# Two transformer-like blocks on one core: loads issued a stage earlier, and one gate projection moved by one pass

## What is computed

```
# block 1: mod = silu(c) @ w_mod + b_mod, six parts of 1024
h = x + g1 * gated_deltanet(rmsnorm(x) * (1 + s1) + b1, ctx likewise)   # 8 heads of 128, two directions
u = rmsnorm(h) * (1 + s2) + b2
h = h + g2 * expert_choice_moe(u)        # 16 experts, hidden 2048, 128 tokens each
# block 2, on x1 = rmsnorm(h) * final_g
p = (rmsnorm(x1) * (1 + s1) + b1) @ w_in
y = [ssd_scan(p), windowed_attention(p)] @ w_out          # 8 scan heads, two directions; sinks, 10 chunks
h2 = x1 + g1 * y
out = rmsnorm(h2 + g2 * grouped_top_k_moe(u2))            # 32 experts, hidden 512, several blocks of 128 tokens
```

## Time and profile before

| | us |
|---|---|
| median of 3 runs | 4617.72 |
| lowest and highest run | 4614.37, 4617.97 |
| the profiled execution | 4615.21 |
| its span on the core | 4613.5 |
| mean granted PE clock | 0.943 |
| PE busy | 4118.3 (89%) |
| DVE busy | 1541.0 (33%) |
| ACT busy | 815.6 (18%) |
| POOL busy | 400.3 (9%) |

### The profile page before, as it was taken

The page is one execution under the profiler, slowest core; times in us unless marked ns, Lnnn a source line. Parts: engine busy times, 40 slices in busy tenths (PEclk is TensorE's granted clock), DMA queues, the critical chain, the costliest instruction groups (busy, mean ns, idle before and its releaser), DMA issues. The chain is left out here.

```text
span 4613.5 us, 42680 instructions
## 1 busy us (share of the span) xinstructions
PE 4118.3 (89%) x14684; PEld 2249.2 (49%) x14684; DVE 1541.0 (33%) x3314; ACT 815.6 (18%) x1818; POOL 400.3 (9%) x385
## 2 busy tenths in 40 slices
PE   6699999998777999999999996997798889999984
PEld 4366666666423444444444443544665344444432
DVE  4577777776352000000000004235953310000003
ACT  2223333332110000000000003111163101011002
POOL 0111111111000000000000000002500010000001
PEclk8799999999888999999999997998799989999997
DMA  6111111110467898888888874010012279999986
GB/s 270 50 27 36 41 41 36 41 30 22 167 256 294 310 313 305 304 313 309 306 308 311 308 264 147 24 29 13 1 70 87 80 254 334 334 335 334 336 312 238
DMA packets 437206, 875.43 MB, mean 190 GB/s; under 512 B 89745, under 2 KB 134625, under 8 KB 430921
## 3 DMA queue, kind: packets, MB, share of 16 engines
q1 hardware_dynamic: 410905, 785.86, 48.8%
q0 software_dynamic: 19616, 71.38, 4.6%
q10 hardware_dynamic: 6544, 16.39, 0.9%
HBM read 801.14 MB, written 72.43 MB: 189 GB/s over the span
## 5 line engine op out<-in xcount | busy, mean ns | idle before, releaser
L1707 PE MATMUL moe_gbank<-moe_ring,moe_xT 128*128 128x512 f32 x1536 | 679.9, 596 | 3.8 <-ACTq L1763 3.8
L1725 PE MATMUL moe_acc<-moe_ring,moe_hidT 128*128 128x512 f32 x1536 | 675.1, 592 | 1.8 <-DVEq L1824 1.1
L1707 PE MATMUL moe_ubank<-moe_ring,moe_xT 128*128 128x512 f32 x1536 | 675.1, 592 | 0.0
L1797 DVE TENSOR_TENSOR moe_hid<-moe_sg,moe_ubank 128x512 f32<-128x512 f32 x96 | 66.0, 688 | 1632.4 <-PE moe_ubank L1707 1632.4
L799 PE MATMUL gdn_pbank<-mix_xT,gdn_w 128*128 128x512 f32 (+1 forms) x1280 | 541.2, 557 | 2.6 <-PEq L693 2.6
L1707 PEld LDWEIGHTS moe_gbank<-moe_ring,moe_xT 128*128 128x128 f32 x1536 | 293.5, 191 | 373.7 <-issue 370.5
L1725 PEld LDWEIGHTS moe_acc<-moe_ring,moe_hidT 128*128 128x128 f32 x1536 | 288.2, 190 | 347.1 <-issue 347.1
L1707 PEld LDWEIGHTS moe_ubank<-moe_ring,moe_xT 128*128 128x128 f32 x1536 | 284.5, 190 | 322.4 <-issue 322.4
L1768 ACT ACTIVATE moe_sg<-moe_gbank 128x512 f32<-128x512 f32 x96 | 57.3, 597 | 1547.6 <-PE moe_gbank L1707 1547.6
L799 PEld LDWEIGHTS gdn_pbank<-mix_xT,gdn_w 128*128 128x128 f32 x1280 | 229.6, 194 | 161.3 <-issue 152.8
L2146 PE MATMUL proj_abank<-mix_yT,mix2x_wq 128*128 128x512 f32 x416 | 180.8, 592 | 0.6 <-PE proj_abank L2146 0.6
(11 more groups left out here) (523 smaller groups left out, 4769.9 us busy)
## 6 DMA issues: line engine op xcount, KB each, us to landing
moe_ring<-in_moe_w_gate SPq DMA_DIRECT2D x64, 2048.0 KB, 7.9
moe_ring<-in_moe_w_up SPq DMA_DIRECT2D x64, 2048.0 KB, 8.2
moe_ring<-in_moe_w_down SPq DMA_DIRECT2D x64, 2048.0 KB, 8.0
moe_ring<-in_w_gate SPq DMA_DIRECT2D x32, 2048.0 KB, 10.5
moe_ring<-in_w_up SPq DMA_DIRECT2D x32, 2048.0 KB, 9.8
moe_ring<-in_w_down SPq DMA_DIRECT2D x32, 2048.0 KB, 10.1
front_wt<-in_w_mod SPq DMA_DIRECT2D x24, 1024.0 KB, 13.8
route_wt<-in_w_ada SPq DMA_DIRECT2D x24, 1024.0 KB, 15.6
```

Of the source, the lines that this page charges most:

```text
L1707: last = nc.tensor.matmul(bank[:], xT[:, k, :], w[:, k * 512:(k + 1) * 512], start=(k == 0), stop=(k == KD - 1))
L1725: last = nc.tensor.matmul(acc[j][:], hidT[:, k, :], w[:, k * D + j * 512:k * D + (j + 1) * 512], start=(f == 0 and k == 0), stop=(f == NF ...
L1797: nc.vector.tensor_tensor(hid[:], sg[:], ubank[:], ALU.mult).then_inc(u_free, 1)
```

## The change

1. The gate projections of head 0 move from iteration 0 into iteration -1, into the same gaps 20 to 27. Iteration 0 has none; from iteration 1 on nothing changes. ACT's SiLU of them moves with them.
2. In iteration 7 SP loads the eight parts of `w_out` when z1 of head 7, the last reader of xT, is done, into xT's space. The wait for the stores leaves `delta_net`; out1's SP waits for them before its load of yk[7], and loads only yk.
3. moe1's last result is computed in a tile of its own at the top of the program (`y_last`, 4 KB in each partition, in front of every other tile but three). POOL no longer waits for the last scatter; n34's SP does, before its loads of x2 and x3, which now come after all six parameters. DVE waits for gain, scale 1 and shift 1, scales, norms the two context tiles, and only then waits for the other three.
4. `project`'s SP issues `a_log`, `dt_bias`, `cap`, `d_skip` and `ssd_norm` before its own loads, and waits for them at its end. tabs and ssd load nothing; `tri` is taken from the top of the program.
5. attention's SP issues, after its own three loads, the 8 loads of w_out_2 and the router's seven. out2 loads no weights; route has no SP block.
6. The stages are nested anew; three that had no semaphores have one or two, and so a block of clears at their end.

The diff, cut to its core:

```diff
 def projections(i):
-    if 0 <= i < H:
-        names += [(f"z{j}", i) for j in range(2)]
+    if i != 0:
+        names += [(f"z{j}", max(i, 0)) for j in range(2)] if i < H else []
...
 # delta_net, SP
+                    if i == H - 1:
+                        sp.wait_ge(p_full, P_AT["z1", i])
+                        for k in range(KD):
+                            sp.dma_start(w_next[:, k, :], w_out[k * P:(k + 1) * P, :]).then_inc(w_ahead, 16)
...
-                sp.wait_ge(y_stored, 16 * H)
...
 # out_norm, SP and PE
                     if yT is None:
+                        if k == KD - 1:
+                            sp.wait_ge(y_stored, 16 * H)
                         sp.dma_start(yk[:, k, :], yT_d[k]).then_inc(w_loaded[k], 16)
-                    sp.dma_start(w[:, k, :], w_out[k * P:(k + 1) * P, :]).then_inc(w_loaded[k], 16)
+                    if w_here is None:
+                        sp.dma_start(w[:, k, :], w_out[k * P:(k + 1) * P, :]).then_inc(w_loaded[k], 16)
...
+                if w_here is not None:
+                    pe.wait_ge(w_ahead, 16 * KD)
                 for k in range(KD):
-                    pe.wait_ge(w_loaded[k], 32 if yT is None else 16)
+                    if yT is None:
+                        pe.wait_ge(w_loaded[k], 16)
...
 # norms_and_narrow, SP and DVE
-                sp.dma_start(gb, row_view(gain)).then_inc(par_loaded, 16)
-                for i in (1, 0):
-                    sp.dma_start(sc[i], row_view(shift_scale[i][1])).then_inc(par_loaded, 16)
-                    sp.dma_start(sh[i], row_view(shift_scale[i][0])).then_inc(par_loaded, 16)
-                    if i:
-                        for t in range(NC_T, NB):
-                            load_x(t)
-                        sp.dma_start(g0, row_view(g_first)).then_inc(par_loaded, 16)
+                sp.dma_start(gb, row_view(gain)).then_inc(ctx_loaded, 16)
+                sp.dma_start(sc[1], row_view(shift_scale[1][1])).then_inc(ctx_loaded, 16)
+                sp.dma_start(sh[1], row_view(shift_scale[1][0])).then_inc(ctx_loaded, 16)
+                sp.dma_start(g0, row_view(g_first)).then_inc(par_loaded, 16)
+                sp.dma_start(sc[0], row_view(shift_scale[0][1])).then_inc(par_loaded, 16)
+                sp.dma_start(sh[0], row_view(shift_scale[0][0])).then_inc(par_loaded, 16)
+                sp.wait_ge(scattered, 16)
+                for t in range(NC_T, NB):
+                    load_x(t)
...
-                dve.wait_ge(par_loaded, 96)
-                for i in (1, 0):
-                    nc.vector.scalar_tensor_tensor(out=sc[i], in0=sc[i], scalar=1.0, in1=gb, op0=ALU.add, op1=ALU.mult)
+                dve.wait_ge(ctx_loaded, 48)
+                nc.vector.scalar_tensor_tensor(out=sc[1], in0=sc[1], scalar=1.0, in1=gb, op0=ALU.add, op1=ALU.mult)
                 dve.drain()
                 for t in range(NC_T):
                     second(t)
+                dve.wait_ge(par_loaded, 48)
+                nc.vector.scalar_tensor_tensor(out=sc[0], in0=sc[0], scalar=1.0, in1=gb, op0=ALU.add, op1=ALU.mult)
+                dve.drain()
...
 # project, SP
+                for tile, rows in scan_parts:
+                    sp.dma_start(tile, rows).then_inc(scan_loaded, 16)
...
+                sp.wait_ge(scan_loaded, 16 * len(scan_parts))
...
 # attention, SP
                 sp.dma_start(snk[:], row_view(sinks)).then_inc(setup, 16)
+                load_next(sp)
...
 # second_block
+            w_next, w_ahead = s1.sb("w_next", [P, KD, D]), s1.sem("w_ahead")
+            def load_next(sp):
+                for k in range(KD):
+                    sp.dma_start(w_next[:, k, :], a["w_out_2"][0][k * P:(k + 1) * P, :]).then_inc(w_ahead, 16)
...
 # program
+        y_last, scattered = top.sb("y_last", [P, D]), top.sem("scattered")
```

More of the change, by code:

```diff
@@ L1250, in tiles_of, with out_norm @@
     return (s, NC_T - 1 - s if s < NC_T else NA - 1 + NC_T - s)
-def out_norm(nc, name, yT_d, w_out, gate, res_rows, h_rows, shift, scale, gain, ident, uT, rows_out, yT=None):
+def out_norm(nc, name, yT_d, w_out, gate, res_rows, h_rows, shift, scale, gain, ident, uT, rows_out, yT=None, w_here=None, w_ahead=None, y_stored=None):
     NBANK = 4
@@ L1257, in out_norm @@
     with Stage(nc, name) as st:
-        w = st.sb("w", [P, KD, D])
+        w = st.sb("w", [P, KD, D]) if w_here is None else w_here
         yk = st.sb("yk", [P, KD, L]) if yT is None else yT
@@ L2271, in scan_tables @@
         with nc.Block() as block:
-            @block.sync
-            def _(sp):
-                sp.dma_start(al[:].rearrange("p d h -> p (d h)"), row_view(a_log.rearrange("d h -> (d h)"))).then_inc(loaded, 16)
-                sp.dma_start(dtb[:].rearrange("p d h -> p (d h)"), row_view(dt_bias.rearrange("d h -> (d h)"))).then_inc(loaded, 16)
             @block.tensor
@@ L2399, in rows @@
                             h = 4 * half + q
-                            last = nc.tensor.matmul(b[:, q * P:(q + 1) * P], dA[:, t, d, h:h + 1].broadcast_to([P, P]), tri[:, d, :], start=True, stop=True)
+                            last = nc.tensor.matmul(b[:, q * P:(q + 1) * P], dA[:, t, d, h:h + 1].broadcast_to([P, P]), tri[:, d * P:(d + 1) * P], start=True, stop=True)
                         last.then_inc(d_full, 1)
@@ L2723, in _, with route @@
                     divide(u)
-def route(nc, hT, w_group, b_group, w_expert, b_expert, cst, ident, ones, idxT, wgt, dest, ebk):
+def route(nc, hT, router, loaded, ident, ones, idxT, wgt, dest, ebk):
     NE = NG + E2
@@ L3150, in second_block @@
-def second_block(nc, a, cst, ident, ones, tri, mod2, h_d, out):
+    with Stage(nc, "ffn1") as ff:
+        idxT, gateT = ff.sb("idxT", [P, E1], U32), ff.sb("gateT", [P, E1])
+        with Stage(nc, "first") as top:
+            xT = top.sb("xT", [P, KD, TOK])
+            w_next = xT[:].rearrange("p k n -> p (k n)")[:, 0:KD * D].rearrange("p (k n) -> p k n", k=KD)
+            w_ahead, y_stored = top.sem("w_ahead"), top.sem("y_stored")
+            with Stage(nc, "mix1") as st:
+                tab = st.sb("tab", [P, H, KINDS, NU])
+                front(nc, consts, (a["w_mod"][0], a["b_mod"][0], a["c"][0], a["c_ctx"], mod1), tile_rows(a["ctx"][0]) + tile_rows(a["x"][0]), a["norm_mix_g"][0],
+                      a["gdn_w_in"][0], a["gdn_a_log"][0], a["gdn_dt_bias"][0], cst, ident[:], xT, tab)
+                delta_net(nc, xT, a["gdn_w_in"][0], a["gdn_conv_w"][0], a["gdn_o_gain"][0], tab, cst, ident[:], ones[:], yT_d, a["gdn_w_out"][0], w_next, w_ahead, y_stored)
+            with Stage(nc, "ffn1r") as s2:
+                uT = s2.sb("uT", [P, KD, L])
+                out_norm(nc, "out1", yT_d, a["gdn_w_out"][0], mod1[0, D6[2]], tile_rows(a["x"][0]), tile_rows(h_d),
+                         mod1[0, D6[3]], mod1[0, D6[4]], a["norm_ffn_g"][0], ident[:], uT, tile_rows(u_d), w_here=w_next, w_ahead=w_ahead, y_stored=y_stored)
+                expert_choice(nc, uT, a["moe_w_router"][0], ident[:], idxT[:], gateT[:], job2)
+        experts(nc, "moe1", E1, F1 // 512, 6, a["moe_w_gate"][0], a["moe_w_up"][0], a["moe_w_down"][0], u_d, idxT[:], ident[:], h_d, gateT=gateT[:], gate=mod1[0, D6[5]], y_last=y_last, last_out=scattered)
@@ L3151, in dram, with second_block @@
+def second_block(nc, a, cst, ident, ones, tri, mod2, h_d, out, scattered):
     def dram(name, shape, dt=F32):
@@ L3184, in second_block @@
-            attention(nc, qT, kT, vtok, a["attn_sinks_2"][0], cst, ident[:], yT2, tile_rows(y_buf)[E2:])
+                scan_tables(nc, dtr[:], al, dtb, tri[:], ones[:], *tv)
+                state_scan(nc, BC, Btok, xs, z, *tv, dsk, nrm, cap, tri, ident[:], yT2)
+            NE = NG + E2
+            wr, br, iota, strict, tokf = (s1.sb(n, [P] + w) for n, w in (("wr", [KD, NE]), ("br", [NE]), ("iota", [P]), ("strict", [P]), ("tokf", [NT])))
+            router_loaded = s1.sem("router_loaded")
@@ new lines, in second_block @@
+            w_next, w_ahead = s1.sb("w_next", [P, KD, D]), s1.sem("w_ahead")
+            def load_next(sp):
+                for k in range(KD):
+                    sp.dma_start(w_next[:, k, :], a["w_out_2"][0][k * P:(k + 1) * P, :]).then_inc(w_ahead, 16)
+                cc = const_columns()[0]
+                with nc.allow_non_contiguous_dma("narrow rows"):
+                    sp.dma_start(wr[:, :, 0:NG], a["w_group_2"][0].rearrange("(k p) n -> p k n", p=P)).then_inc(router_loaded, 16)
+                    sp.dma_start(wr[:, :, NG:], a["w_expert_2"][0].rearrange("(k p) n -> p k n", p=P)).then_inc(router_loaded, 16)
+                    sp.dma_start(br[:, 0:NG], row_view(a["b_group_2"][0])).then_inc(router_loaded, 16)
+                    sp.dma_start(br[:, NG:], row_view(a["b_expert_2"][0])).then_inc(router_loaded, 16)
+                for tile, name in ((iota, "iota"), (strict, "strict"), (tokf, "token")):
+                    at, n = cc[name]
+                    sp.dma_start(tile[:], cst[:, at:at + n]).then_inc(router_loaded, 16)
```

102 lines of the change are left out of this document (33 added, 69 removed).

## The result

The changed kernel takes 4590.57 us (median of 5 runs, 4587.28 to 4594.10) against 4617.72 before; the ratio is 0.9944, with a 95% interval of 0.9933 to 0.9955. It is faster by 27 us, between 21 and 31. The forecast was 4581 with a range of 4568 to 4596: the sign and the range hold, and of the 36.7 us of the sum about three quarters came. Two things that the prediction had named as signs against it are there, though: block two's first load still comes 9 us behind the scatter, and PE has a new wait for the gate weights.

The account below looks back on a forecast made before the run. PE was taken to bound the kernel, busy 4118.3 of 4613.5 us; the other 495 are in reach. Terms −14.3 −4.0 −2.3 −4.7 −5.05 −2.35 −5.2 +1.2 = −36.7 from 4615.2, plus 2.5 for the median, give 4581; range 4568 to 4596.

Parts of the forecast that it names:

- rival C: Transition to block two: the block's end waits for the scatter anyway, only the split's 6.7 us remain; 4588.6 us, chance 0.22.
- the clock not kept: Start of the second output projection: PE's clock does not stay at 2.4 GHz, +2.35 us; with a late scatter 4591.
- Part 2: First output projection: store wait moved behind other loads (−2.3) and one transfer needed for the first product (−1.7), together −4.0 us.
- Part 3: Tables and scan: small loads issued earlier, so the tables gain −2.3 us and the scan −4.7 us.
- Part 5: Delta net: head 0's gate products move into the preparation; price 0, gain 0, ends −1 and +2 us.
- the bound of +2: Iteration 0's tail: with fewer products PE's clock may fall and lengthen the DVE, PE, DVE chain, up to +2 us.
- Rival B: Iteration 0's tail: the moved gate products pay as well, PE's 13.7 us come back; 4567 us, chance 0.08.
- Part 1: Transition from experts to block two: SP starts 7.6 us earlier, DVE waits 6.8 less; −14.3 us, ends −11 and −16.
- Part 4: Second output projection and router: weight wait gone (−5.05), clock stays at 2.4 GHz (−2.35), router's wait gone (−5.2 us).
- 0, at most +1: Attention: cost of issuing the next stages' loads there, behind attention's own three in SP's queue, in us.
- Rival D: Expert products: the new 4 KB tile moves later tiles and slows PE's reads; +51 us at 2.5%, 4632 us, chance 0.02.
- the 1.2 for the clears: Three stages get an end with a block of clears, about 0.4 us each: +1.2 us, 0 to +2.9.

Follow-up runs that it names:

- runs 2 and 3: Head 0's gate products put back in iteration 0 of the changed kernel: 4589.90 us (0.9939); that move alone in the kernel before: 4615.87 us (0.9994).
- runs 4 and 5: Changed kernel with the last scatter issued in block two's first stage: 4590.58 us (0.9939); with no last scatter: 4557.37 us, other data, not compared.
- run 6: Changed kernel with PE's wait for the weights split in block two's first stage, gate weights awaited only before their first product: 4591.76 us (0.9944).
- run 7: Changed kernel with PE's wait for the weights split and x4 loaded ahead of the gate weights: 4595.24 us (0.9955).
- Run 8: Changed kernel with attention's loads for the next stages issued only after the fourth unit's softmax: 4595.16 us (0.9943).
- runs 9 and 10: Kernel before with an unused tile of 4224 bytes per partition at the bottom of SBUF, twice: 4621.76 us (1.0003) and 4621.36 us (single execution).

## Why the prediction was right, and by how much it was off

The sign and the range were right, but the time is nearer to rival C (4589, or 4591 with the clock not kept) than to the forecast's 4581. It lies inside the prediction's own ends (4575 to 4595), although the first term alone missed its worse end of −11 by 5 us: parts 2 and 3 came in full, 4 us above the worse ends that the sum had allowed for. That C's 4591 is met almost exactly is luck: C had the start of block two unmoved and all of the split's 6.7 us, and neither is what the runs show.

**Part 2, out1: right**, −4.05 against −4.0. The row of the second projection priced a first load (5.13) to within 0.07 us.

**Part 3, tables and scan: right**, −7.0 in every execution.

**Part 5, the gate products: right.** Its price is 0, shown by runs 2 and 3, its cover shrank to 9.1 us (8.9 forecast), and the clock of the tail fell, as the bound of +2 allowed. Head 0's result is stored 127.7 to 129.3 us after the sums of squares where the move is in, and 127.6 to 128.2 where it is not, 0.7 us apart on the mean. Rival B is out.

**Part 1, the transition: the step that failed.** "With the wait moved behind the parameters, SP starts at about 2791.2 + 1.7": it started 1.6 us earlier, not 7.6. Two errors: the end of the block waits for the scatter in any case (3.9 us, runs 4 and 5; that was rival C, held at 0.22), and the 1.7 us for the turn of the stage was too small (2.1 us). The prediction had taken it from the clears alone; 4.8 from copy to load is the measure, and no row shown of the kernel before gave it. With −5.9 for both parts the term came out beyond its own worse end. The split of the parameters did its part on DVE (6.05 of 6.8 us), but PE's products moved by only 4.3. For the five transfers the row's 1.37 us each had given 9.9 us and the run shows 10.67. The Trainium skill, "DMA: Bandwidth & Descriptors", section "Anatomy of one DMA", would put them at an estimated 8.0, by a fit for GpSimd's path; the measurement decides, and is further from it than from the row. The prediction named the gate weights as the next thing that might be late, and gave them cover; they did become PE's new wait, but that cost nothing (run 6). What was late was x4: SP's issue of those weights stands ahead of it and ACT's order ties the first tile to x4's squares. Putting x4 first gave 1.0 to 1.7 us (run 7, one execution) of the 1.6 that are left when DVE's 0.8 is taken off.

**Part 4, out2 and the router: the wait went, its surroundings changed.** The load's 5.13 us are gone, but attention up to there is about 2.4 us longer than the removed wait leaves it (−2.7 where −5.1 was due): "0, at most +1" was too small. DVE has its band 1 us later, and PE stays longer at the low level (19 to 20 us instead of 16). Run 8, one execution, has the 2.4 us back; that the loads cause them rests on it alone. The clock at out2 was the other step: "nearest to that one, so I take the clock to stay at 2.4 GHz". In six of nine executions it fell after 2.34 us of idle time, and the stretch is 130.5 us; in three it stayed, and it is 128.8. So −0.7 or −2.35, and the first is the usual one.

**Nowhere in the sum: the placement.** The delta net is 3.4 us longer, and the pad alone makes it 3.6 longer (runs 9 and 10). Rival D had such an effect, in the wrong place: it put it on PE's reads in the experts, where a product still takes 0.6 us. That it would not turn the sign stands.

**The ledger.** 36.7 − 6.0 (start of block two) − 2.4 (the parameters' landing 0.8, x4 and what else held the stage 1.6) − 3.4 (delta net) + 1.0 (out1 to the last indices) − 2.4 (attention) − 1.7 (clock at out2, usual) = 21.8, and with the 1.2 for the clears, which the stretches already hold and no run shows alone, 23.0. The two profiled spans differ by 24.6, the medians by 27, with an interval from 21 to 31. The rest can't be told from what executions differ by.

Left open: by what the placement slows the delta net (other sizes of pad weren't tried), what holds the stage of the narrow projections once x4 is first, and whether a later issue in attention is a gain on the mean.

## What to carry to other kernels

A wait that is moved past the end of a stage is removed only if nothing else in that end waits for the same thing: look for a stage that ends with such a transfer under way, and if there is none, give the two outcomes like weights. When loads are moved a stage forward, what counts is the queue that they are put into: what stands behind them there, and the first microseconds of the stage that they share. A new tile in front of all others moves every tile behind it, and a stage that the change doesn't touch can pay for that; a pad of the same size in the old kernel shows how much.

## What the runs showed of the hardware that was not expected

- The end of a block waits for a DMA that GpSimd's queue has under way, in the one place of this program where it was tried: 10.3 us from index copy to the next block's first load with the scatter, 4.8 without it, 4.7 with the scatter issued a block later.
- The granted clock after a short idle time isn't set by its length alone. After 2.34 us in front of out2 it went to the 1.2 GHz level in six executions of the changed order and stayed at 2.4 GHz in three, the same kernel among both. The three are those in which it also stayed up in front of `project`, and those whose low level at attention's start lasted longest, until 28 to 31 us after its first product (16 to 21 in the others). In these three the 1.7 us gained at out2 stand beside some 4 to 5 us more in attention. By what the chip decides isn't shown.
- A shift of 4224 bytes in each partition lengthens the delta net by 2.5 to 4.5 us, in both executions that have nothing else changed, and shortens the stretch from out1 to the last indices by 0.9 to 2.8.
